# Modulation rows of a two-block model: the sum over eight row groups made by VectorE, and TensorE adding the partitions of each sum

## What is computed

```python
c_act = jax.nn.silu(c)                       # c: (1, 1024)
for l in range(DEPTH):                       # 2 layers
    mod = c_act @ w_mod[l] + b_mod[l]        # w_mod[l]: (1024, 6144)
    sh1, sc1, gt1, sh2, sc2, gt2 = jnp.split(mod, 6, axis=-1)
    ...
```

```python
def conv_ffn(h, norm_g, w_up, conv_w, conv_b, w_down):
    u = dwconv_centred(rmsnorm(h, norm_g) @ w_up, conv_w, conv_b)
    return (jax.nn.gelu(u[..., :D_FF]) * u[..., D_FF:]) @ w_down
```

## Time and profile before

| | |
|---|---|
| median of 3 runs | 3202.38 us (3201.16 to 3205.64) |
| profiled execution | 3196.41 us, of it span 3194.5 us |
| busy in the span | PE 94%, DVE 50%, ACT 41%, POOL 4% |
| mean granted clock of TensorE | 0.965 |
| first feed-forward phase | about 650 to 1046 us of the span |
| second feed-forward phase | about 1398 to 1791 us of the span |

### The profile page before, as it was taken

One profiled execution on the slowest core, in us unless ns is written; L12 is line 12 of the kernel. 1 busy time (PEld: TensorE's weight loads), 2 busy tenths in 40 slices (PEclk: granted clock), 3 DMA queues, 4 the chain that ended last, 5 costly groups with the idle time before them and its releaser, 6 DMA issues. The chain is left out here.

```text
span 3194.5 us, 50954 instructions
## 1 busy us (share of the span) xinstructions
PE 3014.4 (94%) x21910; PEld 2343.1 (73%) x21910; DVE 1608.7 (50%) x2276; ACT 1296.5 (41%) x1995; POOL 120.1 (4%) x215
## 2 busy tenths in 40 slices
PE   7998787899999999999999999999999999999999
PEld 5764666677777777677777776677888876678887
DVE  5325665455354475745354457744332477543333
ACT  3222433343233443743233444655333436644241
POOL 0200000010000000010000010100000101000000
PEclk9999877899999999999999999999999999999999
DMA  4320000254543222254544231012232320032232
GB/s 145 96 70 12 4 3 4 80 168 139 179 147 120 82 79 99 74 167 130 180 142 139 89 101 57 1 60 86 95 100 95 99 85 1 16 104 93 93 105 79
DMA packets 224240, 289.10 MB, mean 90 GB/s; under 512 B 7967, under 2 KB 163911, under 8 KB 217872
## 3 DMA queue, kind: packets, MB, share of 16 engines
q1 hardware_dynamic: 213728, 226.26, 22.7%
q0 software_dynamic: 8704, 55.39, 5.0%
q10 hardware_dynamic: 1584, 4.19, 0.4%
HBM read 281.62 MB, written 2.10 MB: 89 GB/s over the span
## 5 line engine op out<-in xcount | busy, mean ns | idle before, releaser
L226 DVE TENSOR_TENSOR weights_low_all<-weights,weights_high_all 128x2048 fp32r<-128x2048 f32 x196 | 449.1, 2291 | 569.3 <-ACT weights_high_all L220 561.6
L220 ACT CAST weights_high_all<-weights 128x2048 fp32r<-128x2048 f32 x196 | 373.6, 1906 | 568.8 <-PE ps L234 566.7
L232 PE MATMUL ps<-ffn_h_high,weights_high_all 128*128 128x512 f32 x704 | 278.4, 395 | 0.9 <-DVE weights_low_all L226 0.9
L233 PE MATMUL ps<-ffn_h_low,weights_high_all 128*128 128x512 f32 x704 | 274.9, 391 | 0.0
L234 PE MATMUL ps<-ffn_h_high,weights_low_all 128*128 128x512 f32 x704 | 274.7, 390 | 0.0
L232 PE MATMUL ps<-mlp_h_high,weights_high_all 128*128 128x512 f32 x512 | 200.9, 392 | 0.4 <-DVE weights_low_all L226 0.3
L233 PE MATMUL ps<-mlp_h_low,weights_high_all 128*128 128x512 f32 x512 | 199.6, 390 | 0.0
L234 PE MATMUL ps<-mlp_h_high,weights_low_all 128*128 128x512 f32 x512 | 199.6, 390 | 0.0
L232 PE MATMUL ps<-weights_high_all,mlp_hid_high 128*128 128x512 f32 x512 | 199.2, 389 | 0.0
L233 PE MATMUL ps<-weights_low_all,mlp_hid_high 128*128 128x512 f32 x512 | 199.2, 389 | 0.0
L234 PE MATMUL ps<-weights_high_all,mlp_hid_low 128*128 128x512 f32 x512 | 199.2, 389 | 0.0
(11 more groups left out here) (553 smaller groups left out, 6182.7 us busy)
## 6 DMA issues: line engine op xcount, KB each, us to landing
mod_w<-in_w_mod POOLq DMA_DIRECT2D x48, 1024.0 KB, 5.1
weights<-in_ffn_w_up SPq DMA_DIRECT2D x88, 512.0 KB, 5.0
weights<-in_w_mlp_in SPq DMA_DIRECT2D x32, 1024.0 KB, 5.5
weights<-in_w_mlp_out SPq DMA_DIRECT2D x32, 1024.0 KB, 4.9
weights<-in_ffn_w_down SPq DMA_DIRECT2D x24, 768.0 KB, 4.5
weights<-in_mix_w_in SPq DMA_DIRECT2D x13, 1024.0 KB, 5.2
weights<-in_na_w_qkv SPq DMA_DIRECT2D x12, 1024.0 KB, 5.1
weights<-in_w_in SPq DMA_DIRECT2D x12, 1024.0 KB, 5.3
```

What stands on the lines that cost most here:

```text
L220: nc.scalar.copy(st.high[s][:], st.raw[s][:]).then_inc(st.high_done, 1)
L226: nc.vector.tensor_tensor(st.low[s][:], st.raw[s][:], st.high[s][:], ALU.subtract).then_inc(st.split_done, 1)
L232: nc.tensor.matmul(out, lh, rh, start=start, stop=False)
L233: nc.tensor.matmul(out, lh, rl, start=False, stop=False)
```

## The change

The sum over the row groups k moves from PE to DVE. `w_mod[l]` is loaded with k running fastest: all eight row groups of one column group follow one another. Two of the four buffers now take the loads (`SLOTS = 2`), the other two (`SUMS = 2`) hold sums, r = 0 and r = 2 in the first and r = 1 in the second. `accumulate` on DVE scales a tile by column k of `c_act` (k = 0, `tensor_scalar`) or scales it and adds it to the sum (k = 1 to 7, `scalar_tensor_tensor`, in place). It is called 24 times per layer: behind the low part of the hidden tile in the up groups 2 to 9 of the first up phase and 1 to 8 of the second (`MOD_UP_SUMS`), and in all eight groups of the first down phase, behind the low split or, in the last group of a half, behind the additions. PE's `step` is left three times per layer, once for each sum: behind down group 3 of the first down phase, up group 4 of the second up phase and down group 3 of the second down phase. Its stationary operand is a 128x32 piece of a matrix of ones, its moving operand the sum; it adds the partitions. POOL's loads wait for DVE's sums (`added`).

```diff
-UP_STEPS = (1, 3, 5, 6, 7, 9)
-DOWN_STEPS = (0, 1, 2, 3, 4, 5)
+MOD_UP_SUMS = (range(2, 10), range(1, 9))
+MOD_UP_STEPS = ((), (4,))
+MOD_DOWN_STEPS = ((3,), (3,))
...
             nc.vector.tensor_tensor(self.hid[1][:, g, :], u[1][:], self.hid[0][:, g, :], ALU.subtract).then_inc(self.low_done, 1)
+            if g in MOD_UP_SUMS[self.turn]:
+                self.modulation.accumulate(dve)
...
-            if self.modulation and g == self.n - 2:
+            if self.modulation and not self.first and g == self.n - 2:
                 self.modulation.add(dve)
             if g % self.nq < self.nq - 1:
+                if self.modulation and self.first:
+                    self.modulation.accumulate(dve)
                 continue
...
                 nc.vector.tensor_tensor(here, here, sums, ALU.add).then_inc(self.added, 1)
+            if self.modulation and self.first:
+                self.modulation.accumulate(dve)
...
-    SLOTS = 4
+    SLOTS = 2
+    SUMS = 2
...
-    def load(self, pool, w, turned):
+    def load(self, pool, w):
 
 
         for n in range(self.GROUPS * self.l, self.GROUPS * (self.l + 1)):
-            if n % self.GROUPS == 2:
-                pool.wait_ge(turned, KT)
             if n >= self.SLOTS:
-                pool.wait_ge(self.used, n - self.SLOTS + 1)
-            k, r = (n % self.GROUPS) // 3, n % 3
+                pool.wait_ge(self.added, n - self.SLOTS + 1)
+            r, k = n % self.GROUPS // KT, n % KT
             self.nc.gpsimd.dma_start(self.slots[n % self.SLOTS][:],
                                      w[self.l, k * P:(k + 1) * P, r * 2048:(r + 1) * 2048]).then_inc(self.landed[n % self.SLOTS], 16)
+
+    def accumulate(self, dve):
...
+        n = self.summed
+        r, k = n % self.GROUPS // KT, n % KT
+        src, total, c = self.slots[n % self.SLOTS], self.slots[self.SLOTS + r % 2], self.c_act[:, k:k + 1]
+        dve.wait_ge(self.landed[n % self.SLOTS], 16 * (n // self.SLOTS + 1))
+        if n == 0:
+            dve.wait_ge(self.c_done, 1)
+        if k == 0:
+            if r == 2:
+                dve.wait_ge(self.used, 3 * self.l + 1)
+            else:
+                dve.wait_ge(self.turned, KT)
+            self.nc.vector.tensor_scalar(total[:], src[:], c, None, ALU.mult).then_inc(self.added, 1)
+        else:
+            dve.wait_ge(self.added, n)
+            self.nc.vector.scalar_tensor_tensor(out=total[:], in0=src[:], scalar=c, in1=total[:], op0=ALU.mult, op1=ALU.add)\
+                .then_inc(self.added, 1)
+        self.summed += 1
...
     def step(self, pe):
+
+
         n = self.made
-        k, r = (n % self.GROUPS) // 3, n % 3
-        if n == 0:
-            pe.wait_ge(self.c_done, 1)
-        pe.wait_ge(self.landed[n % self.SLOTS], 16 * (n // self.SLOTS + 1))
+        r = n % 3
+        pe.wait_ge(self.added, KT * (n + 1))
         for j in range(4):
-            mm = self.nc.tensor.matmul(self.cx.ps[32 * j:32 * j + 32, 4 + r, :],
-                                       self.c_act[:, k:k + 1].to_broadcast([P, 32]),
-                                       self.slots[n % self.SLOTS][:, j * 512:(j + 1) * 512], start=(k == 0), stop=(k == KT - 1))
+            mm = self.nc.tensor.matmul(self.cx.ps[32 * j:32 * j + 32, 4 + r, :], self.cx.ones[:, 0:32],
+                                       self.slots[self.SLOTS + r % 2][:, j * 512:(j + 1) * 512], start=True, stop=True)
         mm.then_inc(self.used, 1)
         self.made += 1
```

More of the change, by code:

```diff
@@ L847, with __init__ @@
 class Down:
-    def __init__(self, nc, cx, ctx, tag, up, splits, turn, gate=None, gated=None, squares=False, out=None, modulation=None):
+    def __init__(self, nc, cx, ctx, tag, up, splits, turn, gate=None, gated=None, squares=False, out=None, modulation=None, first=False):
         def sem(name):
@@ L854, in __init__ @@
         self.up, self.hid, self.splits, self.turn = up, up.hid, splits, turn
-        self.gate, self.gated, self.squares, self.out, self.modulation = gate, gated, squares, out, modulation
+        self.gate, self.gated, self.squares, self.out, self.modulation, self.first = gate, gated, squares, out, modulation, first
         self.nq = len(splits)
@@ L955, in feed_forward_phase, with up_step, down_step, step @@
     modulation = cx.modulation
-    def up_step(pe, g):
-        if modulate and g in UP_STEPS:
+    def up_step(pe, half, g):
+        if modulate and g in MOD_UP_STEPS[half]:
             modulation.step(pe)
-    def down_step(pe, g):
-        if modulate and g in DOWN_STEPS:
-            modulation.step(pe)
+    def down_step(half):
+        def step(pe, g):
+            if modulate and g in MOD_DOWN_STEPS[half]:
+                modulation.step(pe)
+        return step
     with nc.Block() as block:
@@ L984, in _ @@
                 up.group(pe, g, lambda j: up.free(pe, g - 2, j) if g >= 2 else None)
-                up_step(pe, g)
-            down.tensor(pe, down_step)
+                up_step(pe, 0, g)
+            down.tensor(pe, down_step(0))
             up = ups[1]
@@ L3176, in __init__ @@
         self.used = ctx.enter_context(nc.semaphore("mod_used"))
+        self.added = ctx.enter_context(nc.semaphore("mod_added"))
         self.bias_in = ctx.enter_context(nc.semaphore("mod_bias_in"))
         self.sig, self.c_done = ctx.enter_context(nc.semaphore("mod_sig")), ctx.enter_context(nc.semaphore("mod_c_done"))
-        self.made = 0
+        self.made, self.summed = 0, 0
     def open(self, scope, l):
         self.l = l
-        self.slots = [scope.enter_context(self.nc.sbuf_tensor(f"mod_w{l}{s}", [P, 2048], F32)) for s in range(self.SLOTS)]
+        self.slots = [scope.enter_context(self.nc.sbuf_tensor(f"mod_w{l}{s}", [P, 2048], F32)) for s in range(self.SLOTS + self.SUMS)]
     def bias(self, pool, b):
@@ L3412, in ffn @@
                             [m.slots[2 + t // 2][:, t % 2 * D:t % 2 * D + D] for t in range(TT)])
+                m.turned = norm.turned
                 ups, downs = [], []
                 for q in range(2):
-                    ups.append(ConvUp(nc, cx, hx, f"fu{l}{q}", l, h, q, hid, u, 11 * q))
+                    ups.append(ConvUp(nc, cx, hx, f"fu{l}{q}", l, h, q, hid, u, 11 * q, m))
                     downs.append(Down(nc, cx, hx, f"fd{l}{q}", ups[q], (3, 3, 3, 2), 2 if q == 0 else 0, squares=(q == 1),
-                                      modulation=m if q == 1 else None))
+                                      modulation=m, first=(q == 0)))
                 def modulate(pool):
                     m.bias(pool, d["b_mod_2"])
-                    m.load(pool, d["w_mod_2"], norm.turned)
+                    m.load(pool, d["w_mod_2"])
                 feed_forward_phase(nc, cx, norm, ups, downs, modulate)
```

10 lines of the change are left out of this document (5 added, 5 removed).

## The result

The kernel with the change takes 3150.83 us as a median of 4 runs (3147.2 to 3153.08), the kernel before beside it 3202.7 us (3201.16 to 3205.64). The ratio is 0.9838, with a 95% interval of 0.9824 to 0.9851: 52 us less, between 48 and 56. The forecast was 3151 us, in a range of 3143 to 3162.

The account below looks back on a forecast made before the run. PE was taken to bound the kernel, busy without a gap in the feed-forward phases; 42 removed steps x 1.22 us = 51.2 us, plus 0 (0 to 1) us, off the 3202.4 us median gave 3151 us, range 3143 to 3162.

Parts of the forecast that it names:

- What bounds the kernel: In the two feed-forward phases PE is busy throughout, so every microsecond taken from PE shortens the program if DVE stays ahead.
- The price of a step: One modulation step of four matmuls delays PE's ordinary matmuls by 1.22 us; removing 42 saves 51.2 us.
- The fused instruction: DVE's multiply-add over 128x2048 float32 takes 2350 ns, bounds 2291 and 3000.
- The plain scaling: Six of DVE's 48 new instructions; may be faster than the fused multiply-add (483 ns for 512 elements), at most the same.
- The room of DVE: In up groups 1.1 us stay free before the tap, 1.5 before the low split; the sum's instruction may take 3.45 us.
- The place without margin: Second down group behind an up phase: split ends 0.04 us before PE needs it; at worst 0.11 us, four times.
- The waits that the change adds: DVE waits for tiles, gpsimd loads for the sum two before, remaining steps for earlier sums; nothing added to the path.
- Rival 1: DVE becomes the bound in 28 up groups, its fused form at half rate (3.95 or 4.7 us): 3165 to 3186 us; 4%.
- Rival 2: Tiles land late, so sums and the splits queued behind them on DVE hold PE: slower, 3210 us; 2%.
- Rival 3: Part of the steps' time stays as PE waits at group boundaries where splits come late: 3156 to 3175 us; 4%.
- The signs named: Profile after: 48 modulation records, groups 10.88 us apart, fused 2.3 to 2.4 us, DVE +110 us, each phase 25.6 us shorter.

## Why the prediction was right, point by point

**What bounds the kernel.** Right. PE stays busy for the whole of the stretches, and the steps removed and put back move the time by what they take on PE.

**The price of a step.** Right: 1.22 us estimated, and 1.21 (change), 1.219 (idle steps put back), 1.217 (last six taken out) measured. The row of the instruction itself, 604 ns for each of 8 records, says neither this nor anything that adds up to it. What gave the number was the start of the ordinary matmuls around it, and it held for steps whose stationary operand is a matrix of ones.

**The fused instruction.** Right: 2350 ns by 512 elements' row and the slope of another operation, 2345 measured, with bounds of 2291 and 3000. **The plain scaling** was only bounded, "at most the same", and takes 1279 ns, a little over half. So the six of them cost DVE 7.7 us and not 14.1, and altogether DVE is busy for 98.5 us more and not for 113. That term was mis-sized and hung on nothing: it lies beside PE's work. (42 x 2.345 + 6 x 1.279 are 106.2 us; the records overlap their neighbours by some 0.08 us, as 710.66 + 2.34 and 712.92 above, and the subtractions around them are counted shorter by that.)

**The room of DVE.** Right in kind, low in size. The forecast had 1.1 us beside the tap (and 1.5 beside the split); the trace after shows 1.33 of idle time, and the experiment with three more instructions 1.43. The term that was off is the limit for the instruction of the sum, 3.45 us there, 3.8 by the experiment. Part of the 0.3 us is that DVE's instructions start under 0.1 us before the record of the one ahead ends, which the forecast, adding 0.02 between two, did not count.

**The place without margin.** Here 0 was taken and 1 us kept, for four places of 0.11. The trace shows at this place (start, us, what)

```profile
790.18 0.39 PE L235 MATMUL ps<-weights_high_all,ffn_hid_low 128*128 128x512 f32 x1
790.41 0.46 PE L233 MATMUL ps<-weights_high_all,ffn_hid_high 128*128 128x512 f32 x1
790.71 0.39 PE L234 MATMUL ps<-weights_low_all,ffn_hid_high 128*128 128x512 f32 x1
```

The split ends at 788.02 + 2.29 = 790.31, 0.10 us ahead of the group. Its first matmul starts on time, 0.23 us behind the last, and the second comes 0.30 behind it, 0.07 more than usual. The first one's record is 0.46 us, between the 0.39 of an undisturbed one and the 0.50 behind a real wait. Four places make 0.28 us: "0" was wrong by that, within the 1 us. It also closes the sum of the phase: 21 steps of 1.219 us less 2 x 0.07 are 25.46 us, and 25.45 were measured.

**The waits that the change adds.** Right. Landing takes 5.0/5.3/8.4 us, against 4.9/5.1/8.4, and no sum waits for a tile. The remaining steps need no wait either; the first of the six:

```profile
812.04 0.39 PE L235 MATMUL ps<-weights_high_all,ffn_hid_low 128*128 128x512 f32 x1
812.36 1.06 PE L3252 MATMUL ps<-mod_w,ones 128*32 128x512 f32 x8
813.36 0.50 PE L233 MATMUL ps<-weights_high_all,ffn_hid_high 128*128 128x512 f32 x1
813.69 0.39 PE L234 MATMUL ps<-weights_low_all,ffn_hid_high 128*128 128x512 f32 x1
```

The gap from 812.04 to 813.36 is 1.32 us and the next 0.33, the same picture as in the earlier trace rows.

**The three rivals.** Rival 1 did not come, because the instruction runs at full rate. The experiment with three more instructions shows that its mechanism and its place (waits of PE for the low split in up groups) were right. Rival 2 did not come: even one buffer, with sums up to 4 us late in the down groups, costs PE 0.13 us in a phase. Rival 3 did not come beyond the 0.07 us at four places. The Trainium skill, Vector Engine (DVE) Microarchitecture Reference, Points that are easy to get wrong, gives the fused form with two SBUF sources that aren't bf16 half the throughput. It does not say half of what. This case meets both conditions: 2345 ns for 2048 elements and 750 for 512 are 1.04 ns for each further one. That is the slope of a plain subtraction of two tensors, so against it nothing is halved, and the reading on which the prediction built this rival fails. Against the scaling of one tensor (1279 and 483 ns, 0.52 for each further element) it is half, and in this reading the trace agrees with the sentence. That the prediction at 512 elements saw a disagreement holds for the first reading alone.

**The signs named.** 48 records, 10.88 us between the groups, 2.3 to 2.4 us for the fused instruction, one wait of 0.94 us in the phase: all as said. The 25.6 us for a phase were 25.45 and 25.41. DVE's "some 110 us more" were 98.5, because of the plain scaling and the overlap of the records. That the forecast of 3151 us meets the median of 3150.83 to 0.2 us is partly luck: the four runs lie within 5.9 us, a further five of the same kernel have a median of 3149.84, and the gain came out as 51.9 and 53.2 us between the medians, for the 51.2 forecast and the 50.9 of the two phases. The choice to take the shift of the sum from the median and not from the profiled execution mattered: from the latter, 3196.41 - 51.2 = 3145.2, the forecast would have been 5.6 us too low.

## What to carry to other kernels

Where an engine is busy without a gap, the price of work on it is how much later its ordinary instructions start behind it, not the duration in the row of the work, and it can be checked by taking it out or putting idle copies in. Before moving work to another engine, follow that engine's chain through one period, find who is needed next and how long it idles there: here it was 1.1 us read ahead of the run and 1.43 by experiment, and moved work was free up to that. Beyond it each group paid the excess (0.63 us in 20 of 28 groups), except where PE had work of its own to give the time back. When two profiled executions don't agree with the medians, compare a stretch that begins and ends at the same events in both, and leave the rest to the runs' spread.

## What was not expected of the hardware

- The fused multiply-add over 128x2048 (2345 ns) takes 56 ns more than a plain subtraction of two tensors of that size (2289), and the scaling of one tensor by a column takes 1279 ns, 55% of it.
- Four matmuls of 32 stationary columns and 512 moving in float32 cost an unbroken stream of PE 1.22 us, five and a third of its ordinary matmuls of 128 columns (0.227 us each).
- Where the low split ended just in time, at four places, PE's second matmul came 0.07 us late, though no wait is on record. Behind a step or a wait on record the first matmul's record is 0.50 us long, and the second comes 0.33 to 0.34 behind it, so 0.11 more than usual.
- DVE at 80% busy in a stretch with more loads (DMA share 0.60 against 0.49) left the modulation tiles' landing at a median of 5.3 us. The weights of the up groups, which SP issues, landed in 5.8 us as a median after, against 5.0 before; PE noticed none of it. The two rows, of after and of before (tile, queue, count, KB each, median us to landing):

```profile
weights<-in_ffn_w_up SPq DMA_DIRECT2D x88, 512.0 KB, 5.8
```

```profile
weights<-in_ffn_w_up SPq DMA_DIRECT2D x88, 512.0 KB, 5.0
```
